# Inputs laid out on the host in the order of their use, in one fused transformer-like block on one core

## Time and profile before

| | us |
|---|---|
| median of 3 runs | 734.14 (733.96 to 734.96) |
| span of the profiled execution | 734.8 |
| PE busy | 562.5 (77%) |
| PE weight loads busy | 341.6 (46%) |
| DVE busy | 204.6 (28%) |
| ACT busy | 73.0 (10%) |
| POOL busy | 44.1 (6%) |
| data moved | 242.44 MB in 46098 packets, 330 GB/s |

### The profile page before, as it was taken

The page is one execution under the profiler, slowest core; times in us unless marked ns, Lnnn a source line. Parts: engine busy times, 40 slices in busy tenths (PEclk is TensorE's granted clock), DMA queues, the critical chain, the costliest instruction groups (busy, mean ns, idle before and its releaser), DMA issues.

```text
span 734.8 us, 7708 instructions
## 1 busy us (share of the span) xinstructions
PE 562.5 (77%) x3321; PEld 341.6 (46%) x3321; DVE 204.6 (28%) x433; ACT 73.0 (10%) x139; POOL 44.1 (6%) x68
## 2 busy tenths in 40 slices
PE   7999999999999989899383484594566558447485
PEld 6888888888886646263140141141123114114142
DVE  3898979897112143000010010000000001001002
ACT  3201020202100012100000000000000000000002
POOL 5001212202000011000000000000000000000000
PEclk9999999999999999999697796788779679689798
DMA  8992812444494656999999999999999999999981
GB/s 229 388 293 103 295 49 83 146 176 169 176 405 191 228 225 266 413 429 425 429 429 428 426 427 428 427 428 427 429 427 427 428 427 427 429 427 426 417 332 58
DMA packets 46098, 242.44 MB, mean 330 GB/s; under 512 B 9618, under 2 KB 9710, under 8 KB 35822
## 3 DMA queue, kind: packets, MB, share of 16 engines
q1 hardware_dynamic: 45198, 238.77, 80.1%
q10 hardware_dynamic: 864, 3.15, 1.2%
HBM read 240.86 MB, written 1.05 MB: 329 GB/s over the span
## 4 chain that ended last, share of the span: by engine, by line
PE 54%; DMA 42%; DVE 2%; issue 1%; POOL 1%; ACT 0%; POOLq 0%; PEldq 0%; DVEq 0%
PE bank L1144 28%; DMA ring<-in_w_down 13%; DMA ring<-in_w_gate 12%; DMA ring<-in_w_up 8%; PE bank L1385 8%; DMA x_region<-in_w_up 4%; DMA s_region<-in_w_up 4%; PE bank L1393 4%; PE bank L1265 4%; PE bank L1434 2%; PE bank L1122 2%; PE bank L1455 1%; PE bank L1237 1%; PE bank L1252 1%; PE bank L1350 1%
## 5 line engine op out<-in xcount | busy, mean ns | idle before, releaser
L1385 PE MATMUL bank<-ring,z_region 128*32 128x512 f32 x688 | 114.6, 653 | 64.7 <-DMA ring<-in_w_gate 14.1
L1144 PE MATMUL bank<-x_region,ring 128*128 128x256 f32 x688 | 152.9, 381 | 0.0
L1144 PEld LDWEIGHTS bank<-x_region,ring 128*128 128x128 f32 x688 | 129.3, 190 | 22.5 <-issue 4.3
L1385 PEld LDWEIGHTS bank<-ring,z_region 128*32 128x32 f32 x688 | 32.7, 119 | 122.3 <-issue 122.3
L1393 PE MATMUL bank<-ring,m_region 128*32 128x512 f32 x240 | 54.0, 718 | 26.2 <-DMA ring<-in_w_down 15.8
L1059 DVE TENSOR_TENSOR z_region<-z_region,bank 128x512 f32<-128x512 f32 x8 | 8.2, 1028 | 210.6 <-PE bank L1385 198.6
L1385 PE MATMUL bank<-x_region,z_region 128*32 128x512 f32 x80 | 44.8, 723 | 10.8 <-DMA ring<-in_w_up 10.8
L1063 DVE COPY m_region<-bank 128x512 f32<-128x512 f32 x8 | 5.5, 692 | 146.1 <-PE bank L1393 111.9
L1385 PE MATMUL bank<-rot_region,z_region 128*32 128x512 f32 x64 | 36.7, 738 | 10.9 <-DMA ring<-in_w_up 10.9
L1393 PE MATMUL bank<-s_region,m_region 128*32 128x512 f32 x64 | 36.8, 740 | 9.1 <-DMA ring<-in_w_down 9.1
L1350 PE MATMUL bank<-conv_region,h_region 128*128 128x128 f32 x256 | 33.1, 284 | 4.8 <-issue 4.2
(11 more groups left out here) (243 smaller groups left out, 570.1 us busy)
## 6 DMA issues: line engine op xcount, KB each, us to landing
ring<-in_w_gate SPq DMA_DIRECT2D x29, 2048.0 KB, 33.6
ring<-in_w_up SPq DMA_DIRECT2D x20, 2048.0 KB, 33.4
ring<-in_w_down SPq DMA_DIRECT2D x20, 2048.0 KB, 35.8
ring<-in_w_in SPq DMA_DIRECT2D x11, 2048.0 KB, 10.8
s_region<-in_w_up SPq DMA_DIRECT2D x4, 2048.0 KB, 34.2
rot_region<-in_w_down SPq DMA_DIRECT2D x4, 2048.0 KB, 32.4
s_region<-in_w_down SPq DMA_DIRECT2D x4, 2048.0 KB, 36.8
x_region<-in_w_up SPq DMA_DIRECT2D x4, 2048.0 KB, 36.3
```

The costliest lines, as they stand in the source:

```text
L1144: ins = MM(dst, w[:, k, n * P:(n + 1) * P], rhs[:, k, :], start=k == 0, stop=k == kn - 1)
L1385: ins = MM(bank[to][quarter(e), :], xT[:, k, quarter(e)], of_expert[e][:, FF * k:FF * k + FF], start=k == 0, stop=k == KD - 1)
```

## The change

The host packs the inputs into new arrays before the launch (`laid_out`), and the kernel reads these. All short vectors become one array `columns` of 128 x 108, which one transfer brings straight into `cols` (432 bytes per partition); `rows`, the two transposes and the product on PE, and ACT's three copies go, and `keep_clock(1, 4)` becomes `keep_clock(1, 7)`. B and C of the state space come in one transfer each with 2 KB per partition, the router in two. Every mixer unit is one transfer with one run of 16 KB per partition, the pairs and rows of pack 0 and the rows of pack 7 too, the halves have one run of 8 KB. The order in which SP issues the units, the slots and all sizes stay.

```diff
-        rows = sb("rows", [N_ROWS, P])
-        cols = sb("cols", [P, 128])
-        logdt_row = sb("logdt_row", [1, GROUPS])
+        cols = sb("cols", [P, N_COLS])
...
         @block.sync
-            load_rows(((R_GMIX, KD, norm_mix[0]), (R_ARE, ST, a_re[0].rearrange("g n -> (g n)")),
-                       (R_AIM, ST, a_im[0].rearrange("g n -> (g n)"))), rows_in)
-            sp.dma_start(logdt_row[:], log_dt[0:1, :]).then_inc(rows_in, 16)
-            for u, src in enumerate(sources):
+            sp.dma_start(cols[:], columns[:]).then_inc(cols_in, 16)
+            for u in range(MIX_UNITS):
                 if u == 1:
-                    load_rows(((R_CONVW, 3 * KD, conv_w[0].rearrange("a b c -> (a b c)")), (R_CONVB, KD, conv_b[0]),
-                               (R_GATEB, 2 * KD, gate_bias[0].rearrange("a c -> (a c)")),
-                               (R_SSMD, YB, ssm_d[0])), later_rows_in)
-                    for i, part in enumerate((b_re, b_im)):
-                        sp.dma_start(bld[:, i], part[0].rearrange("(t g) n h -> (g n) t h", g=2)).then_inc(b_in, 16)
-                    for i, part in enumerate((c_re, c_im)):
-                        sp.dma_start(cld[:, i], part[0].rearrange("(b g) h n -> (g h) b n", g=8)).then_inc(c_in, 16)
+                    sp.dma_start(bld.rearrange("p i t h -> p (i t h)"), s5_b[:]).then_inc(b_in, 16)
+                    sp.dma_start(cld.rearrange("p i b n -> p (i b n)"), s5_c[:]).then_inc(c_in, 16)
...
-                if u in U_GLU:
-                    for i in range(2):
-                        sp.dma_start(glu_half(u)[:, i], src[i]).then_inc(loaded[u % MIX_RING], 16)
-                else:
-                    sp.dma_start(mix_slot(u).rearrange("p (k n) -> p k n", k=src.shape[1]), src).then_inc(loaded[u % MIX_RING], 16)
+                sp.dma_start(mix_slot(u), mix[u]).then_inc(loaded[u % MIX_RING], 16)
...
                 if what == "pair":
-                    view = gate_v if part % 2 == 0 else up_v
-                    return view[:, experts, (part // 2) * 1024:(part // 2 + 1) * 1024]
+                    return first[part]
                 if what == "rows":
-                    return down_v[:, experts, part * D:(part + 1) * D]
+                    return first[8 + part] if pk == 0 else last_rows[part]
                 if what == "half":
-                    return half_v[:, experts, KF - 1, 512 * part:512 * part + 512]
+                    return last_halves[part]
...
-            pool.wait_ge(cols_ready, 2)
-            nc.gpsimd.tensor_tensor(dt_t[:], eul[:], s5c[:, 0, :], ALU.pow).then_inc(dt_ready, 1)
+            pool.wait_ge(cols_in, 16)
+            nc.gpsimd.tensor_tensor(dt_t[:], eul[:], cols[:, R_LOGDT:R_LOGDT + ST], ALU.pow).then_inc(dt_ready, 1)
...
-            act.wait_ge(cols_psum, 1)
-            nc.scalar.activation(cols[:, FIRST_ROWS], bank[0][:, FIRST_ROWS], ACT.Copy).then_inc(cols_ready, 1)
-            for g in range(2):
-                ins = nc.scalar.activation(s5c[64 * g:64 * g + 64, 0, :],
-                                           bank[0][64 * g:64 * g + 64, 128 + g:128 + GROUPS:2], ACT.Copy)
-            ins.then_inc(cols_ready, 1)
-            act.wait_ge(cols_ready, 2)
+            act.wait_ge(cols_in, 16)
...
             keep_clock(1, 7)
-            pe.wait_ge(rows_in, 16 * 4)
-            nc.tensor.transpose(bank[0][:, FIRST_ROWS], rows[FIRST_ROWS, :], ident[FIRST_ROWS, FIRST_ROWS])
-            MM(bank[0][:, 128:128 + GROUPS], ones[0:1, :], logdt_row[:], start=True, stop=True).then_inc(cols_psum, 1)
-            keep_clock(1, 4)
+            keep_clock(1, 7)
...
-            pe.wait_ge(later_rows_in, 16 * 4)
-            pe.wait_ge(cols_ready, 2)
-            nc.tensor.transpose(bank[0][:, LATER_ROWS], rows[LATER_ROWS, :], ident[LATER_ROWS, LATER_ROWS]).then_inc(cols_psum, 1)
...
+def in_tiles(w, tiles, columns):
+    return w.reshape(tiles, P, columns).transpose(1, 0, 2).reshape(P, tiles * columns)
+
+def laid_out(inputs):
...
+    parts = [0, D, 2 * D, 3 * D + SSM, 3 * D + SSM + D]
+    mix = np.stack([in_part(3 * D)] + [in_part(c0 + 512 * half) for half in range(2) for c0 in parts]
+                   + [conv_out(0), conv_out(1), glu(0), out_rows(0), glu(1), out_rows(1)])
...
+    gate, up = pack_of("w_gate", 0, 4), pack_of("w_up", 0, 4)
+    pairs = np.stack([gate, up], axis=1).reshape(8, P, UNIT)
+    first = np.concatenate([pairs, pack_of("w_down", 0, KF).reshape(KF, P, UNIT)])
+    last = pack_of("w_down", PACKS - 1, KF)
+    halves = last[KF - 1].reshape(P, PACK, 2, 512).transpose(2, 0, 1, 3)
```

More of the change, by code:

```diff
@@ L64 @@
 MASKED = -1.0e30
-R_GMIX, R_ARE, R_AIM, FIRST_ROWS = 0, 8, 24, slice(0, 40)
-R_CONVW, R_CONVB, R_GATEB, R_SSMD, LATER_ROWS = 64, 88, 96, 112, slice(64, 116)
-N_ROWS = 116
+R_GMIX, R_ARE, R_AIM, R_LOGDT, R_CONVW, R_CONVB, R_GATEB, R_SSMD, N_COLS = 0, 8, 24, 40, 56, 80, 88, 104, 108
 EVEN_BANKS, ODD_BANKS = (0, 1, 4, 5), (2, 3, 6, 7)
@@ L99, in mixer_schedule, with block_kernel @@
     return order
-def block_kernel(nc, x_in, norm_mix, w_in, conv_w, conv_b, w_conv_out, a_re, a_im, log_dt, b_re, b_im,
-                 c_re, c_im, ssm_d, w_glu_a, w_glu_b, gate_bias, w_o, norm_ffn, w_rg, b_rg, w_re, b_re_,
+def block_kernel(nc, x_in, columns, mix, s5_b, s5_c, norm_ffn, route_w, route_b, first, last_rows, last_halves,
                  w_gate, w_up, w_down, norm_final, out):
@@ L343, in transfers_to @@
         def transfers_to(slot, units):
-            return sum(2 if u in U_GLU else 1 for u in units if u % MIX_RING == slot)
+            return sum(u % MIX_RING == slot for u in units)
         def last_mix_unit(slot):
@@ L615, in _ @@
                                      scale=cols[:, R_GMIX + k:R_GMIX + k + 1]).then_inc(hT_act, 1)
-            act.wait_ge(cols_psum, 2)
-            nc.scalar.activation(cols[:, LATER_ROWS], bank[0][:, LATER_ROWS], ACT.Copy).then_inc(cols_ready, 1)
             act.wait_ge(angle_ready, 1)
@@ L1301, in _ @@
                         ins.then_inc(h2T_psum, 1)
-            pe.wait_ge(route_in, 64)
+            pe.wait_ge(route_in, 32)
             for k in range(KD):
@@ L1503, in _ @@
             combine(0, PACKS, last=True)
-_INS = ["x", "norm_mix", "w_in", "conv_w", "conv_b", "w_conv_out", "ssm_a_re", "ssm_a_im", "ssm_log_dt",
-        "ssm_b_re", "ssm_b_im", "ssm_c_re", "ssm_c_im", "ssm_d", "w_glu_a", "w_glu_b", "gate_bias", "w_o",
-        "norm_ffn", "w_route_group", "b_route_group", "w_route_expert", "b_route_expert", "w_gate", "w_up",
-        "w_down", "norm_final"]
+def in_tiles(w, tiles, columns):
+    return w.reshape(tiles, P, columns).transpose(1, 0, 2).reshape(P, tiles * columns)
@@ new lines, in laid_out, with column, in_part, conv_out @@
+def laid_out(inputs):
+    import numpy as np
+    one = {name: np.asarray(a)[0] if name not in ("norm_final",) else np.asarray(a) for name, a in inputs.items()}
+    def column(vector):
+        return vector.reshape(-1, P).T
+    log_dt = np.repeat(one["ssm_log_dt"].reshape(ST, 2).T, STATE, axis=0)
+    columns = np.concatenate([column(one["norm_mix"]), column(one["ssm_a_re"]), column(one["ssm_a_im"]), log_dt,
+                              column(one["conv_w"]), column(one["conv_b"]), column(one["gate_bias"]),
+                              column(one["ssm_d"])], axis=1)
+    def in_part(c0):
+        return in_tiles(one["w_in"][:, c0:c0 + 512], KD, 512)
+    def conv_out(h):
+        return in_tiles(one["w_conv_out"][:, 512 * h:512 * h + 512], KD, 512)
+    def glu(h):
+        return np.concatenate([in_tiles(one[w][:, 512 * h:512 * h + 512], YB, 512) for w in ("w_glu_b", "w_glu_a")], axis=1)
+    def out_rows(h):
+        return in_tiles(one["w_o"][512 * h:512 * h + 512], 4, D)
+    parts = [0, D, 2 * D, 3 * D + SSM, 3 * D + SSM + D]
+    mix = np.stack([in_part(3 * D)] + [in_part(c0 + 512 * half) for half in range(2) for c0 in parts]
+                   + [conv_out(0), conv_out(1), glu(0), out_rows(0), glu(1), out_rows(1)])
+    s5_b = np.stack([one[b].reshape(ST, P, GH).transpose(1, 0, 2) for b in ("ssm_b_re", "ssm_b_im")], axis=1)
+    s5_c = np.stack([one[c].reshape(YB, P, STATE).transpose(1, 0, 2) for c in ("ssm_c_re", "ssm_c_im")], axis=1)
+    route_w = np.concatenate([one["w_route_group"], one["w_route_expert"]], axis=1).reshape(P, KD * N_LOGITS)
+    route_b = np.tile(np.concatenate([one["b_route_group"], one["b_route_expert"]]), (P, 1))
+    def pack_of(name, pk, parts_of):
+        w = one[name][pk * PACK:(pk + 1) * PACK]
+        return w.reshape(PACK, P, parts_of, -1).transpose(2, 1, 0, 3)
+    gate, up = pack_of("w_gate", 0, 4), pack_of("w_up", 0, 4)
[3 more added lines that the diff above has]
+    halves = last[KF - 1].reshape(P, PACK, 2, 512).transpose(2, 0, 1, 3)
+    return {"x": inputs["x"], "columns": columns, "mix": mix, "s5_b": s5_b.reshape(P, -1), "s5_c": s5_c.reshape(P, -1),
+            "norm_ffn": inputs["norm_ffn"], "route_w": route_w, "route_b": route_b, "first": first,
```

(7 more changed lines are left out.)

28 lines of the change are left out of this document (9 added, 19 removed).

## The result

The changed kernel is slower: 740.66 us median of 6 runs (738.57 to 742.03), beside 735.40 (733.96 to 737.98) of 6 runs of the kernel before; the ratio is 1.0056, with a 95% interval of 1.0037 to 1.0075, so 4.1 us with 2.7 to 5.5. The forecast was +2.1 us and 736.2, with a range up to 738.2. The direction was right, the size was half, and the time lies outside. A part of the distance isn't the change's: the forecast started from the 734.14 us of the first three runs of the kernel before, whose six have 735.40. From 734.14 the measured +4.1 would end at 738.2, on the edge of the range. The profiled execution has a span of 738.4 us, 3.6 over the 734.8 before.

What follows compares the result with a forecast made beforehand. PE's back-to-back mixer work, fixed routing latency, then the saturated expert stream were taken to bound the kernel, so start shifts reach the end nearly whole. +2.5 - 0.2 - 0.2 = +2.1 us on 734.14 gave 736.2 us, range 733.3 to 738.2.

Steps and rivals of the forecast that it cites:

- 7 x 0.62 = 4.3 us more until the second half of x is in: Start: each of x's 7 remaining packets per engine waits for one 16 KB packet of unit 0; PE's transposes +2.5 us.
- the 2.4 under which PE wouldn't have felt it: Start: a second half of x late by less than 2.4 us (11.05 - 8.63) stays hidden behind PE's idle products.
- the term put at nothing: Start: columns' 128 short packets, 8 per engine, were called small and counted as nothing.
- the collision: Start, likeliest case: unit 0's wide packets go between x's packets and delay its second half; 60%, at 736.2 us.
- One packet at a time, in turn: DMA engines: queues q1 and q10 share an engine by alternating single packets, read from x's second load at 202 to 210 us.
- no collision: Start, rival: second half of x late by less than 2.4 us, only idle products count; +0.1, 734.3 us; 22%.
- The prediction's other reading: Start: all 8 wide rows of unit 0 on an engine go in one turn; 4.9 us for x, 736.8 us in the end.
- the +0.5 of the rival: Start: idle products' cover ends at 11.05 instead of 10.51 us, +0.5, if nothing else is later.
- the 0.4 that I kept for the upper end alone: Start: PE's slower clock after the wait for x, 0.4 us, added only to the upper end.
- The stream's -0.2: Pack 0: only its twelfth unit loads in the saturated stream, 4.90 us at 428 GB/s instead of 5.07: -0.2 us.
- the prediction's own sign: Last up unit landing over 1 us earlier relative to pack 0's first unit than before (406.2 us) favours narrow units holding the stream.
- the rate rival: Expert stream, rival: narrow units were holding the saturated stream, 2.7 us would go; 731.8 us or part of it; 11%.

Runs made afterwards that it cites:

- e3: Changed kernel with the experts' old layout (pack 0 and pack 7's rows in 4 KB runs, halves in 2 KB): 740.69 us, ratio 1.0050 to the kernel before.
- e1: Changed kernel, but SP waits until the first half of x has landed before it issues unit 0: 734.62 us, ratio 0.9976 to the kernel before.
- e7: Changed kernel, but SP waits for POOL's clearing of ident (about 3.8 us) before it issues unit 0: 733.13 us, ratio 0.9960 to the kernel before.
- h1: Changed kernel, but SP issues unit 0 only when ACT has issued both halves of x: 733.55 us, ratio 0.9971 to the kernel before.
- f1: Kernel before, with unit 0 alone in rows of 16 KB, still issued at 2.41 us: 736.19 us, ratio 0.9997 to the kernel before.
- g1: Changed kernel, but ACT issues all of x as one transfer, ahead of unit 0's issue: 735.37 us, ratio 0.9991 to the kernel before.
- e4: Changed kernel, but the second half of x is SP's first transfer, ahead of columns and unit 0: 734.78 us, ratio 0.9973 to the kernel before.
- e5: Changed kernel, but SP issues B and C ahead of unit 0 and not behind it: 734.05 us, ratio 0.9956 to the kernel before.
- e6: Changed kernel with 39 idle products ahead of the transposes in place of 14: 739.30 us, ratio 1.0045 to the kernel before.
- e2: Changed kernel with unit 0 alone in 8 runs of 2 KB per partition, issued at the same place: 736.77 us, ratio 1.0007 to the kernel before.
- g2: Changed kernel with all of x in one transfer and unit 0 in runs of 2 KB: 734.44 us, ratio 0.9977 to the kernel before.

## Why the prediction was wrong

**What was right.** The transfer of x was what the change hit, and by unit 0's earlier issue; the packets of the two queues alternate one for one, 15 and 15 in 0.6 us; PE waits for `xn`, and the shift isn't absorbed by the mixer or the routing. PE's wait for it is in the chain, and the layout of packs 0 and 7 was worth nothing, which e3 shows. For B and C, the router and mixer units 1 to 16 it is what the profiles suggest (the mixer took 0.2 us less), but no run took one of them back alone.

**The step that failed** is the size of the term "7 x 0.62 = 4.3 us more until the second half of x is in". It was 5.56. The prediction had 7 packets of x left on each engine when unit 0's first packet comes, from two counts: the packet comes at 3.5 us, and x goes on as in the kernel before, with 121 packets started by 3.3 us, since of columns' 128 short packets "I count nothing". Both were wrong. Unit 0's first wide packet started at 4.10 us. And in the changed kernel's queues from 1.5, from 2.1 and from 2.7 us stands:

```profile
q1 hardware_dynamic: 18, 0.01, 34.1%
q10 hardware_dynamic: 3, 0.01, 9.3%
...
q1 hardware_dynamic: 7, 0.00, 6.0%
...
q10 hardware_dynamic: 45, 0.18, 74.5%
q1 hardware_dynamic: 71, 0.03, 20.3%
```

x has started 3 + 0 + 45 = 48 packets by 3.3 us and not 121 (in that row 118 are of x and 3 are small ones). By 4.10 it has 126, where the kernel before had 194. So 130 are left, 8 for each engine, and all 128 wide packets of unit 0 start before the last of x. Had x been as far as before, 62 would have been left, about 4 for each engine: by my estimate 4 x 0.62 = 2.5 us, about the 2.4 under which PE wouldn't have felt it. By this count the term put at nothing, `columns`, made the collision a full one. That 7 came near 8 is luck: the early 3.5 us and the nothing for `columns` offset each other. The last packet of x starts at 10.41 instead of 5.14 us: 5.0 (8 x 0.62) of that are the wide packets, and 0.3 is what x is late with `columns` ahead of it and hardly any of unit 0 in its way (5.37 to 5.43 in e1, e7 and h1). Another 0.3 passes between that last packet and the square (0.87 us, where f1 has 0.55). That x is held back by `columns`, where short rows stood, is read from the traces: in the eleven profiles with `columns` at the head of SP's queue x has 40 to 57 packets by 3.3 us, in the kernel before and f1 118 and 126. No run took `columns` away alone.

**The reason given for the step was only half of it.** "One packet at a time, in turn" holds where both queues have packets. Whether they have them at the same time was taken for granted. g1 and h1 show that the order of issue decides: issued 0.4 to 0.5 us after all of x, unit 0 delays it by 0.1 us at most (h1's second square at 6.04, e1's at 5.95). The prediction asked of the rival "no collision" that unit 0's packets "begin after 4.0 us"; they did, at 4.10, and the collision was full. The moment of that first packet alone doesn't decide; how much of x is still to come by then does. The prediction's other reading, all 8 wide rows of an engine in one turn, is refuted by the 15 and 15. How the packets of two transfers of the same moment are made, and why ACT's queue is empty for a us beside a narrow unit 0 and not beside a wide one, stays open.

**Smaller terms.** The idle products ended at 9.49 us and not at 11.05. The prediction priced them at the 0.48 us that they took in the profile before, where PE ran at its lower clock until 13.7 us; in the changed kernel's profile the clock rose at 8.1 us, in others at other moments (last section), and the 14 products ended between 9.1 and 10.6. So the +0.5 of the rival "no collision" is in none of these profiles, and e1, e4, e5, e7 and h1 are all faster than before. PE's work behind the wait was slower: 3.68 + 3.69 us for the transposes and the first columns against 3.37 + 3.45, at a granted clock of 0.50 (1.2 GHz) from 12 to 18 us: 0.55, near the 0.4 that I kept for the upper end alone. (At 2.4 GHz the transposes take 1.75 us, as e6 shows; the kernel before had them at the lower clock as well.) The routing's 1.15 us was not foreseen (below). The stream's -0.2 was -1.4 in this profile. By the prediction's own sign, more than 1 us, this would give it to the rate rival; but e3 took the layout of the experts back and kept the short stretch (404.5), and f1 shows that most of it is scatter.

In sum on the span: predicted +2.5 - 0.2 - 0.2; measured +4.1 at the projections, -0.2 in the mixer, +1.15, -1.4: +3.6. Of the rivals, "worse" (7%) described a second half of x late by 6.5 us and 738.8 us: nearer than the forecast, though not for its reason, turns of more than one wide packet.

## What to carry to other kernels

Before two queues are given work at the start, look at the moment of issue of the small transfer that everything waits for and of the big one that nobody needs yet: here half a us between them is worth 6 us (1.0056 against 0.9971), more than all the rest of the repacking. Without the collision that rest is 2 to 3 us under the kernel before, and no run tells which part of it (the transposes and copies that went, or a layout) brings them. When a change takes small transfers away from the head of a queue, ask what moves up in their place. A count of packets taken from the old trace is only good if what stood ahead of them stays.

## What was not expected of the hardware

**A clock dip in the routing goes with 1.2 to 1.7 us, whatever the kernel.** From the last w_o products to pack 0's first unit, the 14 profiles fall in two groups: 26.8 us in six (before, e2, e6, g1, g2, e7) and 28.0 to 28.5 in eight (the changed kernel twice, e1, e3, e4, e5, f1, h1). In the first the mean granted clock from 262 to 290 us is 1.00, in the second 0.94. The dip comes while PE works in pieces between DVE's and ACT's steps; the same eight transposes took 1.94 us in the changed kernel and 1.06 before. It isn't tied to the start's wait: h1 has it and e2, which waits at the start, doesn't. So of the changed kernel's 3.6 us in the profile 1.15 may be the dip and not the change: e6, which starts as late, goes without it.

**The clock's first rise comes at another moment in each execution, and the column PEclk doesn't show it.** In the kernel before, 16 transposes of `xn` took 3.37 us. With the same code f1 has

```profile
9.41 1.91 PE L1137 MATMUL bank<-ident,m_region 128*128 128x128 f32 x16
```

The column says 1.00 for both. But the trace's list of clock grants begins only at 13.7 us in the kernel before and at 8.3 in f1, and where nothing is listed yet the column counts full clock. The pace says otherwise: in all 14 profiles PE's products of 128 columns end 0.21 us apart before the first entry of the list, and 0.11 after it wherever such products follow. So PE ran at 1.2 GHz until then. The entry stands at 8.1 us in the changed kernel's first profile and between 7.2 (e7) and 13.7 us (before) in all, though PE begins its idle products at 4.33 in each. What sets the moment no run here shows. It moves the first projections by 1.1 us between two kernels with the same code at this place (16.39 in f1, 17.52 before), so a difference of that size between two rows of the table says little by itself.
